# Recurrent state rows of eight samples: all on GpSimd, with the weight splits and the projection filler dealt out anew

## The reference, cut to what matters

```python
xn = rms_norm(x, norm_in)
u = jnp.einsum('btd,dc->btc', xn, w_in)
...
def step(S, inp):                       # RWKV-7, one token; S is (batch, head, 64, 64)
    r_t, k_t, v_t, kk_t, a_t, w_t = inp
    sa = jnp.einsum('bhij,bhj->bhi', S, kk_t)
    S = (S * w_t[:, :, None, :] - sa[..., None] * (kk_t * a_t)[:, :, None, :]
         + v_t[..., None] * k_t[:, :, None, :])
    return S, jnp.einsum('bhij,bhj->bhi', S, r_t)
```

## Time and profile before

| | us |
|---|---|
| median of three runs | 2529.87 |
| the profiled execution | 2528.83 |
| its span, first to last instruction | 2527.2 |
| PE busy | 2279.9 |
| DVE busy | 1247.1 |
| ACT busy | 796.7 |
| POOL busy | 496.1 |

### The profile page before, as it was taken

The page is one execution under the profiler, slowest core; times in us unless marked ns, Lnnn a source line. Parts: engine busy times, 40 slices in busy tenths (PEclk is TensorE's granted clock), DMA queues, the critical chain, the costliest instruction groups (busy, mean ns, idle before and its releaser), DMA issues. The chain is left out here.

```text
span 2527.2 us, 52263 instructions
## 1 busy us (share of the span) xinstructions
PE 2279.9 (90%) x21510; PEld 2092.9 (83%) x21510; DVE 1247.1 (49%) x2369; ACT 796.7 (32%) x1545; POOL 496.1 (20%) x386
## 2 busy tenths in 40 slices
PE   5999999899999988999999888989689749999996
PEld 4998888788888877999999777778687639999996
DVE  4344545545454453397883287755235415443223
ACT  4334233242333322222221444545123213231111
POOL 0000000000000000011101488899614400000000
PEclk8999999999999999999999889999899868999998
DMA  3221121212122121586775212212659852332332
GB/s 119 94 86 57 58 70 54 69 41 69 53 66 70 49 78 49 165 284 219 255 249 174 91 55 71 76 54 66 211 174 324 286 191 77 127 138 99 105 105 96
DMA packets 129766, 301.72 MB, mean 119 GB/s; under 512 B 26074, under 2 KB 54068, under 8 KB 123796
## 3 DMA queue, kind: packets, MB, share of 16 engines
q1 hardware_dynamic: 89444, 208.85, 25.7%
q0 software_dynamic: 14944, 52.21, 6.1%
q10 hardware_dynamic: 25168, 37.70, 4.6%
HBM read 261.48 MB, written 45.54 MB: 121 GB/s over the span
## 5 line engine op out<-in xcount | busy, mean ns | idle before, releaser
L178 PE MATMUL acc<-xh,w_hi 128*128 128x272 f32 x3008 | 677.4, 307 | 51.2 <-DVE w_lo L161 31.5
L178 PE MATMUL acc<-xl,w_hi 128*128 128x272 f32 x3008 | 635.1, 293 | 0.0
L178 PE MATMUL acc<-xh,w_lo 128*128 128x272 f32 x3008 | 633.7, 293 | 0.0
L178 PEld LDWEIGHTS acc<-xh,w_hi 128*128 128x128 f32 x3008 | 481.6, 194 | 95.6 <-issue 40.3
L178 PEld LDWEIGHTS acc<-xl,w_hi 128*128 128x128 f32 x3008 | 487.1, 194 | 0.0
L178 PEld LDWEIGHTS acc<-xh,w_lo 128*128 128x128 f32 x3008 | 484.0, 194 | 0.0
L161 DVE TENSOR_TENSOR w_lo<-w_raw,w_hi 128x1024 fp32r<-128x1024 f32 x164 | 200.7, 1224 | 418.2 <-ACT w_hi L153 417.1
L153 ACT ACTIVATE w_hi<-w_raw 128x1024 fp32r<-128x1024 f32 x188 | 198.4, 1055 | 292.5 <-PE acc L178 220.7
L1265 DVE SCALAR_TENSOR_TENSOR b_C<-b_rows,b_pos_s,b_C 128x512 f32<-128x512 f32 x240 | 162.4, 744 | 0.0
L970 PEld LDWEIGHTS rbank<-m 64*64 64x64 f32 x3840 | 120.2, 135 | 22.9 <-issue 14.1
L970 PE MATMUL rbank<-m 64*64 64x64 f32 x3840 | 132.3, 220 | 0.8 <-DVE m L586 0.8
(11 more groups left out here) (415 smaller groups left out, 3375.2 us busy)
## 6 DMA issues: line engine op xcount, KB each, us to landing
w_raw<-in_w_all SPq DMA_DIRECT2D x168, 512.0 KB, 3.7
b_rows<-in_cmp_rows SPq DMA_DIRECT2D x128, 256.0 KB, 3.7
m_w<-in_w_mo SPq DMA_DIRECT2D x32, 1024.0 KB, 5.8
w_raw<-in_w_all ACTq DMA_DIRECT2D x20, 512.0 KB, 5.3
tmp_uT<-ub ACTq DMA_DIRECT2D x35, 272.0 KB, 2.2
m_gates<-tmp_uT SPq DMA_DIRECT2D x16, 544.0 KB, 3.8
d_ring<-in_sel_k SPq DMA_DIRECT2D x64, 128.0 KB, 4.8
d_ring<-in_sel_k POOLq DMA_DIRECT2D x64, 128.0 KB, 4.9
```

What stands on the lines that cost most here:

```text
L178: ins = self.nc.tensor.matmul(acc[:, c, 0:HALF], w[:, k % KH, :], x[:, k, c * HALF:(c + 1) * HALF], start=(k == 0 and m == 0), stop=(k == ...
```

## The change

All 64 rows of the state are stepped by GpSimd (`dve_steps` and N_TOP go). Before the first step GpSimd makes only one split, of half 2, and no longer eight. The splits of halves 3 to 22 stand between the steps, and those of 23, 24 and 25 behind the last. GpSimd's first step now waits for one ScalarE result (s_w) and for s_kk; its fourth kind of instruction waits for s_b. ScalarE's three functions for the samples stand right behind its loads. Five VectorE instructions that only the end needs (bonus and gate) move from the start into the units from the eighth on. TensorE runs 16 pieces before the attention, 68 within it, and keeps 12 (halves 21 to 23) for behind it. In the next stage VectorE enters before it makes its first two splits, and no longer after them.

```diff
 def pool_steps(pool, between):
         pool.wait_ge(ready, 1)
-        pool.wait_ge(act_done, 2)
+        pool.wait_ge(act_done, 1)
         pool.wait_ge(state_in, 16)
...
-            link(tt(top(prod), top(S), across(kk, t), ALU.mult))
-            tt(top(S), top(S), across(w, t), ALU.mult)
-            link(row_sums(sa[:, 0:N_TOP]))
-            link(tt(top(prod), down(v[:, t, :]), across(k2, t), ALU.mult))
+            link(tt(prod[:, :, :], S[:, :, :], last_dim(kk, t), ALU.mult))
+            tt(S[:, :, :], S[:, :, :], last_dim(w, t), ALU.mult)
+            link(row_sums(sa[:, :]))
+            if t == 0:
+                pool.wait_ge(ready, 2)
+            link(tt(prod[:, :, :], over_j(v[:, t, :]), last_dim(k2, t), ALU.mult))
...
-    def dve_steps(dve):
...
 def dve_before(dve):
-        dve.wait_ge(act_done, 3)
+        dve.wait_ge(act_done, 2)
         link(vv.reciprocal(ss[:, :], ss[:, :]))
         link(tt(kk[:, :, :], kraw[:, :, :], over_d(ss), ALU.mult))
+        dve.sem_inc(ready, 1)
         link(tt(b[:, :, :], kk[:, :, :], a, ALU.mult))
...
-PROMPT_PIECES, START_PIECES = PIECES * (PROMPT_CHUNKS - KEY_CHUNKS), 32
-POOL_STEPS, N_TOP = 72, 56
+PROMPT_PIECES, START_PIECES, END_PIECES = PIECES * (PROMPT_CHUNKS - KEY_CHUNKS), 16, 12
+POOL_STEPS = 72
...
-    rest = PROMPT_PIECES - START_PIECES
+    rest = PROMPT_PIECES - START_PIECES - END_PIECES
...
-            FIRST_LOWS = START_PIECES // HALF_PIECES
-            LOWS = W.h_ahead - W.h0 - 2 - FIRST_LOWS
+            LOWS = W.h_ahead - W.h0 - 2 - END_PIECES // HALF_PIECES - 2
...
-                while lows[0] < W.h_ahead and (lows[0] - W.h0 - 3 - FIRST_LOWS) * POOL_STEPS <= steps[0] * LOWS:
+                while lows[0] < W.h_ahead and (lows[0] - W.h0 - 4) * POOL_STEPS <= steps[0] * LOWS:
...
-            while lows[0] < W.h0 + 2 + FIRST_LOWS:
-                W.low(pool, lows[0])
-                lows[0] += 1
+            W.low(pool, lows[0])
+            lows[0] += 1
             samples_steps(pool, between)
...
+            samples_act(act)
             background(8)
-            samples_act(act)
-            background(12)
-            samples_root(act)
-            background(START_PIECES)
...
-            samples_dve(dve)
-            state_rows = samples_low(dve)
+            samples_rest = samples_dve(dve)
...
-                if u >= 4 and state_rows:
-                    state_rows.pop(0)()
+                if u >= 8 and samples_rest:
+                    samples_rest.pop(0)()
...
 # attend_samples, VectorE
-            background(4)
             enter(dve)
+            background(4)
```

More of the change, by code:

```diff
@@ L1388, in rwkv_samples @@
     o_done, sent, state_in = sem("s_o_done"), sem("s_sent"), sem("s_state_in")
-    low_chain, low_stepped = sem("s_low_chain"), sem("s_low_stepped")
+    last_dim = lambda t, i: t[:, i, None, :].to_broadcast([P, HD, HD])
+    over_j = lambda t: t[:, :, None].to_broadcast([P, HD, HD])
     over_d = lambda t: t[:, :, None].to_broadcast([P, DEC_T, HD])
@@ L1401, in store @@
         eng.wait_ge(stepped, 1)
-        eng.wait_ge(low_stepped, 1)
         eng.dma_start(A["s_rwkv"], S[:, :, :]).then_inc(sent, 16)
@@ L1412, in act_before @@
         f(w[:, :, :], sw, ACT.Exp, scale=DECAY_SCALE).then_inc(act_done, 1)
+        act.wait_ge(norm_in, 1)
+        f(ss[:, :], ss[:, :], ACT.Sqrt).then_inc(act_done, 1)
         f(gate[:, :, :], g, ACT.Sigmoid).then_inc(act_done, 1)
-    def act_root(act):
-        act.wait_ge(norm_in, 1)
-        nc.scalar.activation(ss[:, :], ss[:, :], ACT.Sqrt).then_inc(act_done, 1)
     def act_after(act):
@@ L1437, in row_sums @@
             while n > 1:
-                link(tt(top(prod)[:, :, 0:n], top(prod)[:, :, 0:n], top(prod)[:, :, n:2 * n], ALU.add))
+                link(tt(prod[:, :, 0:n], prod[:, :, 0:n], prod[:, :, n:2 * n], ALU.add))
                 n //= 2
[L1440 to L1443, removed]
+            return tt(out, prod[:, :, 0], prod[:, :, 1], ALU.add)
         for t in range(DEC_T):
-            link(tt(top(prod), top(S), across(kk, t), ALU.mult))
-            tt(top(S), top(S), across(w, t), ALU.mult)
-            link(row_sums(sa[:, 0:N_TOP]))
-            link(tt(top(prod), down(v[:, t, :]), across(k2, t), ALU.mult))
[L1449 to L1453, removed]
+            link(tt(prod[:, :, :], S[:, :, :], last_dim(kk, t), ALU.mult))
[4 more added lines that the diff above has]
+            link(tt(prod[:, :, :], over_j(v[:, t, :]), last_dim(k2, t), ALU.mult))
+            link(tt(S[:, :, :], S[:, :, :], prod[:, :, :], ALU.add))
+            link(tt(prod[:, :, :], over_j(sa), last_dim(b, t), ALU.mult))
+            link(tt(S[:, :, :], S[:, :, :], prod[:, :, :], ALU.subtract))
+            link(tt(prod[:, :, :], S[:, :, :], last_dim(X[:, t], 0), ALU.mult))
+            last = row_sums(o[:, t, :])
             if t < DEC_T - 1:
@@ L1513, in dve_before, with gated @@
         link(stt(out=k2[:, :, :], in0=k2[:, :, :], scalar=1.0, in1=k, op0=ALU.add, op1=ALU.mult))
-        dve.wait_ge(act_done, 3)
+        dve.wait_ge(act_done, 2)
         link(vv.reciprocal(ss[:, :], ss[:, :]))
         link(tt(kk[:, :, :], kraw[:, :, :], over_d(ss), ALU.mult))
+        dve.sem_inc(ready, 1)
         link(tt(b[:, :, :], kk[:, :, :], a, ALU.mult))
[L1519 to L1523, removed]
-        dve.sem_inc(ready, 1)
-        link.restart()
+        dve.sem_inc(ready, 1)
+        def gated():
+            dve.wait_ge(act_done, 3)
+            link(tt(gate[:, :, :], gate[:, :, :], g, ALU.mult))
+        return [lambda: link(tt(rk[:, :, :], r, k2[:, :, :], ALU.mult)),
+                lambda: link(tt(rk[:, :, :], rk[:, :, :], over_t(2), ALU.mult)),
+                lambda: link(red(bonus[:, :], rk[:, :, :])),
+                lambda: link(tt(rk[:, :, :], v, over_d(bonus), ALU.mult)),
+                gated,
+                link.restart]
     def dve_after(dve):
@@ L1542, in dve_after @@
         tt(o[:, :, :], oc[:, :, :], gate[:, :, :], ALU.mult).then_inc(o_done, 1)
-    return load, store, act_before, act_root, act_after, pool_steps, dve_before, dve_after, dve_steps, o_done
+    return load, store, act_before, act_after, pool_steps, dve_before, dve_after, o_done
 N_TILE = SEQ // P
@@ L1623, in attend_prompt @@
         chain, sent, stored = sem("a_chain"), sem("a_sent"), [sem(f"a_stored{j}") for j in range(2)]
-        load_samples, store_samples, samples_act, samples_root, samples_act_end, samples_steps, samples_dve, samples_dve_end, samples_low, samples_ended = \
+        load_samples, store_samples, samples_act, samples_act_end, samples_steps, samples_dve, samples_dve_end, samples_ended = \
             rwkv_samples(nc, A, ctx)
@@ L1882, in _ @@
             outs(NU - 1)
-            assert not state_rows
             samples_dve_end(dve)
@@ L2287, in select @@
                 link(ts(mb[:, :], rank[:, :], N_SELECT - 0.5, NEG, ALU.is_gt, ALU.mult))
+            enter(dve)
             background(4)
-            enter(dve)
             v.memset(q[:, :, :, :], 0.0).then_inc(zeroed, 1)
```

## The result

The changed kernel takes 2499.3 us (median of four runs, 2493.9 to 2500.7) against 2528.7 (2526.1 to 2530.8) for the kernel before on the same chip: 0.988, with a 95% interval of 0.9863 to 0.9898. Forecast was 2501.0. The profiled execution is the fastest of the four: 2493.9 us, span 2492.2.

The account below looks back on a forecast made before the run. TensorE was 90% busy, the stage's end set by GpSimd's chain. Entry 30.6 us earlier, less 2 us of reordering, nets 28.6: 2528.83 - 28.6 = 2500.2, median 2501 (forecast 2493 to 2509; 8 in 10 within 2488 to 2520).

Parts of the forecast that it names:

- Waits for ScalarE's rounding: GpSimd's stops between steps until ScalarE has rounded a half: 51.3 us before, predicted to go entirely.
- Middle: TensorE from the attention's first product to the first piece behind it: 353.7 us before, predicted 331.4.
- Wait for half 22: TensorE waiting behind half 21 for GpSimd's split of half 22: predicted 8 us, off the path.
- From half 23 to the entry: TensorE's end of half 23 to the next stage's start: ScalarE's copy and root, then VectorE's normalising, 1763.9 to 1771.6.
- Rival C: More is won: chain takes 317 us, reordering hidden, raw load meets fewer transfers; 2491 us, chance 0.12.
- VectorE's reordering: VectorE's first two splits of the next stage now stand behind the entry: predicted 2 us late.
- Entry: Start of the next stage, behind the state's chain and normalisation: predicted at 1771.6, moved by 30.6 us.
- the transfers set the pace: Next stage's start: loads begin on entry and TensorE follows them, so the entry's gain passes on unchanged.
- the 51.3 us: GpSimd's 8 waits for ScalarE's rounding before the change, put down to asking ahead of TensorE after ten early splits.
- My smallest margin: Split of half 7, behind GpSimd's twelfth step instruction: predicted done 6 us before TensorE wants it.
- rival A: TensorE's slow attention rows came from its clock, not VectorE, so the middle doesn't speed up: 2519 us, chance 0.18.
- Rival D: GpSimd's chain grows by what its earlier start wins, its end staying at 1795: 2545 us; B and D together 0.08.

Follow-up runs that it names:

- e9: The changed kernel run again unaltered, beside three others on their chip: 2499.6 us, ratio 0.9885 to the kernel before.
- e2: The kernel before with VectorE's instructions for state rows 56 to 63 left out, those rows not stepped: 2499.2 us, ratio 0.9891.
- e10: The changed kernel with the state stored by GpSimd right behind its last subtraction, no longer by SyncE: 2499.0 us, ratio 0.9882.
- e6: The changed kernel with no pieces kept for behind the attention, all between its rows: 2505.6 us, ratio 0.991.
- e11: The changed kernel with half 3 split early, bonus instructions at the start, all remaining splits between steps, state stored early by GpSimd: 2514.0 us, ratio 0.995.
- e12: As e11, with 15 pieces ahead of the attention for 16: 2506.1 us, ratio 0.9917 to the kernel before.
- e7: The changed kernel with half 3 split ahead of GpSimd's first step: 2499.2 us, ratio 0.9886 to the kernel before.
- e5: The kernel before with all 64 state rows on GpSimd and nothing else of the change: 2526.2 us, ratio 0.9995.
- e1: The changed kernel with state rows 56 to 63 back on VectorE: 2542.5 us, ratio 1.0051 to the kernel before.
- e3: The changed kernel with its last product done three times, 17.9 us more in GpSimd's chain: 2515.0 us, ratio 0.9953.
- e8: The changed kernel with ScalarE's root of the normalisation ahead of its last pieces' copy: 2498.0 us, ratio 0.9888.

## Why the prediction was right

The mechanism held, and most steps by their size. That the sum came within 2 us is in part luck, since slips of 3 to 8 us up and down cancel each other out. From t0, predicted and then measured:

- First step 14.8, 14.4. Instruction of 4096 elements 8.9, 8.8 to 9.0 us. Attention's start 34.5, 34.2, with a wait of 12.8, 12.2 us ahead of half 3.
- Waits for ScalarE's rounding between first step and chain's end: none expected, none found. The chain ended at 381.8, 378.5 (e9: 379.8): 3 us less, near the lower value that I had for four steps (317).
- Middle 331.4, 335.6 us (e9: 339.7). The 29.8 us between before and e2 are the 32.4 that I took from the rows' excess. What I put at 4 us, the five moved VectorE instructions, shows as one wait of 5.7 us: the copy that TensorE needed stood behind the first product below, while a like one took 0.47 us. A second row (below) cost about 5 us more. Timeline of VectorE:

```profile
1452.39 6.87 DVE L1482 TENSOR_TENSOR s_rk<-s_rk,stab 128x256 f32<-128x256 f32 x1
...
1468.28 0.47 DVE L1484 TENSOR_TENSOR s_rk<-sx,s_bonus 128x256 f32<-128x256 f32 x1
```

- Wait for half 22: 8, 0.9 us (e9: none). Chain earlier, middle longer; the two slips cancel each other out, since GpSimd and TensorE ended together and not GpSimd last.
- From half 23 to the entry: 7.7, 11.1 us (half 22 starts at 1743.23, so half 23 ends 12.2 later, at 1755.4; entry 1766.5). This term was mis-sized. I had ended it with VectorE's work, as before. Now it ends with the state's 2 MB store, which stands on SyncE's queue behind the loads of the next halves. (The four loads ahead of it took 11.5 us to issue, since a load waits until a split has freed its buffer.) Queue of SyncE, then the store's time to landing:

```profile
1743.20 11.54 SPq L146 DMA_DIRECT2D w_raw<-in_w_all  x4
1755.39 0.62 SPq L1403 DMA_DIRECT2D out_s_rwkv<-sS  x1
```

```profile
out_s_rwkv<-sS SPq DMA_DIRECT2D x1, 2048.0 KB, 9.9
```

The chain ended at 1744.7, the store was issued at 1755.4 and had landed at 1765.3. ScalarE's store of the last chunk, issued at 1756.3 beside it, took 9.5 us and landed at 1765.8; by the trace the two can't be told apart as what the entry waited for. In e10 both are out of the way: entry 2.9 us earlier than e9. Rival C had counted on this store being done 20 us ahead of the entry; it landed 1.2 us ahead.
- VectorE's reordering: 2, 2.8 us. Its first two splits of the next stage start 0.7 and 3.5 us behind the entry, for 2.1 ahead of it and 0.7 behind it. No run changes this alone.
- Entry 402.4, 400.3 (e9: 402.7). That is 32.8 and 30.4 us earlier than before, for 30.6 predicted, and the time fell by 29.4 (e9: 27.7) for 28.6.

How the entry goes on into the time shows in the columns "entry" and "t0 to last" of the table, which are of one execution each. Ordered by entry: 449.3 goes with 1174.1 us, 433.1 with 1158.0, 430.5 with 1152.1, 421.7 with 1146.6, 415.2 with 1140.8, 410.6 with 1137.7, 406.7 with 1135.0, 403.3 with 1127.1. From 449.3 to 403.3 the 46.0 us of entry are 47.0 of time, as I had taken it. Below that almost nothing passes on: 403.2, 402.7, 400.3 (twice), 399.8 and 398.9 go with 1127.8, 1128.2, 1126.0, 1126.3, 1127.2 and 1126.7. The forecast entry of 402.4 lies just where the passing on ends, so the prediction's "the transfers set the pace" holds up to it and no further. In the changed kernel's trace, 0.9, 3.8 and 1.8 us of waits are left to TensorE there. That this floor is TensorE's own work on halves 24 to 28 is my reading of those waits; no run makes that work shorter.

Two readings were too simple, and the runs correct them. First, I put the 51.3 us down to splits asked for ahead of TensorE. e2 shows that 20 of them went with VectorE's rows alone. That the order matters as well, the three kernels with a split every 3.3 step instructions instead of 3.8 suggest: the same rows are on GpSimd, and 8.6 (e6), 23.7 (e11) and 15.5 us (e12) of waits are back, where the changed kernel, e7, e9 and e10 have none. e11 loses 14.4 us against e9. Each of the three differs in something else too, so the spacing alone was not tested. My smallest margin was 6 us; that the closer splits use it up is my reading and not shown. Second, rival A (the slow rows come from the clock) is out as the main cause: e2 has 0.98 for 0.94 with only VectorE's instructions gone, so the clock followed the waits. Its part is the longer busy time: 14 of the 30 us in e2. The long rows of the changed kernel show the same order of events. One takes 25.0 us (1560.3 to 1585.3) at PEclk 0.93 between rows of 20 at 1.00, with VectorE no busier than beside it; but TensorE first waited 3.0 us in it, for a copy that ScalarE made behind a chunk's copy and a rounding:

```profile
1569.68 0.49 PE L1879 MATMUL a_bank<-a_kT,a_q 64*128 64x128 f32 x4 [3.00 <-ACT a_PT L1756]
```

```profile
1560.00:1585.00 25.00, 21.82 (x156) 19.25 (x155) 10.18 (x46) 11.21 (x42) 24.61 (x8) 0.93 0.23 59
```

In windows of 2.5 us PEclk is 1.00 up to 1570.0, then 0.71 and 0.60, and 1.00 again from 1575.0. Around the 5.7 us wait it is 0.50 from 1455.0 to 1465.0.

Rival D, the chain's growth eating its earlier start, is what e5 does without the earlier start: the same chain's end as before and no gain. That the growth costs is right; "GPSIMD Engine Reference", section 4.1, of the Trainium skill would leave these rows on VectorE for it. Its factor of two agrees with the trace: from 3584 to 4096 elements GpSimd takes 1.1 us more (7.8, 8.9), 2.1 ns each, and from 256 to 512 VectorE takes 0.26 more (0.43, 0.69), 1.0 ns each; my 1.35 ns held a fixed part. e1 follows that rule and takes 2542.5 us. The page "SBUF — State Buffer" of the Trainium skill (section "SBUF: two separate sides") has the reason, two engines that lock each other out for a whole instruction, and the 3984 ns of e1's products against 690 undisturbed agree.

What the 12 pieces bring beyond 6 us, and which of the early start's parts (one split ahead, one ScalarE result, VectorE's order) gives how much of its 36 us, was not taken apart.

## What to carry to other kernels

Two engines that share a lock are not two workers: moving an eighth of the state from VectorE to GpSimd cost GpSimd 30 us and gave TensorE 30, because the attention's copies stood behind the locked instructions. Such a gain is worth nothing while the longer chain sets the end (e5), and an earlier start is worth nothing while the lock stays (e1), so weigh the two as one change. And when filler work stands in a long chain, compare when each piece may start with when it is asked for: the margin decides. Here the kernels with 3.8 instructions between splits had none of these waits, apart from one of 2 to 3 us in e3 and in e8, and those with 3.3 had 9 to 24 us.

## What the runs showed of the hardware that I had not expected

A short VectorE instruction beside a long one of GpSimd takes nearly as long as that one. The product below has 256 elements; one of that size took 0.47 us above. It starts with GpSimd's first step and ends just past it, at 1389.67 for 1389.39:

```profile
1380.59 9.08 DVE L1475 TENSOR_TENSOR s_b<-s_kk,sx 128x256 f32<-128x256 f32 x1
```

Not every VectorE instruction was held up. Its eight sums over the rows, with one input of 128x512, took 0.68 us each beside the same GpSimd work, in e1 as in the kernel before:

```profile
L1477 DVE TENSOR_REDUCE s_sa<-s_prod 128x8 f32<-128x512 f32 x4 | 2.7, 680 | 0.0
```

But one input is no safeguard: a scaling of four elements a partition (VectorE, L1493, at 1745.22) took 1.89 us beside GpSimd's split and ended with it at 1747.1, where the like one took 0.17 in the kernel before, with GpSimd idle.

And the price is no property of the instruction: VectorE's same 36 cost the middle 30 us in the kernel before (against e2) and 52 in e1 (against the changed kernel). They took 80 us there and 97 in e1, and TensorE waited 19.1 and 33.3 us for the copies behind them. Why they took longer in e1 the runs do not tell.
